# Two later layers of a two-block transformer: low halves of the weights on VectorE alone, head-norm weights in tables and copies, the compressed attention projection computed feature-major

## The reference

```
for l in range(2):
    h = rmsnorm(x, ln_mix[l])
    z = h @ w_in[l]
    (c_q 384, c_kv 128, k_rope 32, fnet 256, dq 256, dk 256, dv 256,
     hq 256, hi 256, hf_fwd 256, hf_bwd 256, hg 256, gate_logits 4096) = split(z)
    # MLA: q = rmsnorm(c_q, g_qa) @ w_uq;  k_nope, v = rmsnorm(c_kv, g_kva) @ w_ukv
    #      q, k = rmsnorm per head of 96 (g_qn, g_kn), then rope on the last 32 columns
    # diff: dq, dk: rmsnorm per head of 32 (g_qn, g_kn), rope; two softmaxes subtracted
    # hgrn: f = lb + (1 - lb) * sigmoid(hf); k = 1 - f; log f is summed along time
    # fnet: a 2-D DFT of fnet
    x = x + (sum over 4 branches of sigmoid(gate) * (o_branch @ w_branch)) @ w_out[l]
    x = x + (silu(h2 @ w_g) * (h2 @ w_u)) @ w_down[l],  h2 = rmsnorm(x, ln_ffn[l])
```

## Time and profile before

| | |
|---|---|
| median of 3 runs | 1344.58 us (1338.54 to 1344.88) |
| the profiled execution, its own time | 1347.75 us |
| its span from first to last instruction | 1346.0 us |
| mean granted TensorE clock | 0.991 |
| PE / PEld / DVE / ACT / POOL busy | 1292.8 / 1188.1 / 919.1 / 621.8 / 219.8 us |

### The profile page before, as it was taken

One profiled execution on the slowest core, in us unless ns is written; L12 is line 12 of the kernel. 1 busy time (PEld: TensorE's weight loads), 2 busy tenths in 40 slices (PEclk: granted clock), 3 DMA queues, 4 the chain that ended last, 5 costly groups with the idle time before them and its releaser, 6 DMA issues.

```text
span 1346.0 us, 22062 instructions
## 1 busy us (share of the span) xinstructions
PE 1292.8 (96%) x9180; PEld 1188.1 (88%) x9180; DVE 919.1 (68%) x1261; ACT 621.8 (46%) x1005; POOL 219.8 (16%) x175
## 2 busy tenths in 40 slices
PE   8999989999988899999999999999899998999998
PEld 7987959998877889998899998788899998999987
DVE  6868646664469977699675554579876997655553
ACT  5865445553354455343354443445463442544432
POOL 2100000000015730282000000056402730000000
PEclk9998999999999999999999999999999999999999
DMA  9522425555533424332545555434233434455552
GB/s 373 209 94 95 173 92 180 188 188 189 189 118 120 164 94 142 140 126 95 187 153 185 186 184 201 156 126 157 96 126 125 157 126 156 158 188 188 188 188 94
DMA packets 30323, 211.76 MB, mean 157 GB/s; under 512 B 3344, under 2 KB 3728, under 8 KB 5264
## 3 DMA queue, kind: packets, MB, share of 16 engines
q1 hardware_dynamic: 29936, 210.22, 43.7%
q10 hardware_dynamic: 288, 0.13, 0.0%
HBM read 209.29 MB, written 1.05 MB: 156 GB/s over the span
## 4 chain that ended last, share of the span: by engine, by line
PE 71%; DVE 18%; issue 5%; ACT 4%; POOL 1%; DMA 0%; DVEq 0%; ACTq 0%
PE bank L471 69%; DVE W L1441 1%; DVE stat L1385 1%; DVE w_lo L1469 1%; DVE x_lo L1578 1%; DVE stat L1386 1%; DVE stat L1387 1%; ACT w_hi L1024 1%; PE bank L744 1%; DVE W L1795 1%; DVE xs L1961 1%; DVE W L1428 1%; PE bank L555 1%; DVE junk L1959 1%; POOL w_lo L981 1%
## 5 line engine op out<-in xcount | busy, mean ns | idle before, releaser
L1469 DVE TENSOR_TENSOR w_lo<-ring,w_hi 128x2048 fp32r<-128x2048 f32 x157 | 366.5, 2334 | 261.1 <-ACT w_hi L1024 260.9
L1024 ACT ACTIVATE w_hi<-ring 128x1024 fp32r<-128x1024 f32 (+1 forms) x364 | 361.9, 1044 | 222.9 <-PE bank L471 211.5
L471 PE MATMUL bank<-x_hi,w_lo 128*128 128x256 f32 x1776 | 248.5, 282 | 7.4 <-POOL w_lo L981 6.3
L471 PE MATMUL bank<-x_hi,w_hi 128*128 128x256 f32 x1776 | 253.7, 284 | 0.1
L471 PE MATMUL bank<-x_lo,w_hi 128*128 128x256 f32 x1776 | 247.6, 280 | 2.2 <-DVE x_lo L1578 2.2
L471 PEld LDWEIGHTS bank<-x_hi,w_lo 128*128 128x128 f32 x1776 | 226.0, 189 | 9.5 <-POOL w_lo L981 7.2
L981 POOL TENSOR_TENSOR w_lo<-ring,w_hi 128x1024 fp32r<-128x1024 f32 (+1 forms) x48 | 115.7, 2414 | 703.3 <-ACT w_hi L1024 701.4
L471 PEld LDWEIGHTS bank<-x_hi,w_hi 128*128 128x128 f32 x1776 | 227.4, 189 | 2.2 <-DVE x_hi L1566 0.7
L471 PEld LDWEIGHTS bank<-x_lo,w_hi 128*128 128x128 f32 x1776 | 225.3, 188 | 4.2 <-DVE x_lo L1578 3.9
L471 PE MATMUL bank<-W 128*128 128x128 f32 (+4 forms) x716 | 122.4, 329 | 9.4 <-DMA const<-constants 5.7
L471 PEld LDWEIGHTS bank<-W 128*128 128x128 f32 (+3 forms) x716 | 96.1, 188 | 25.9 <-issue 6.6
(11 more groups left out here) (240 smaller groups left out, 1350.7 us busy)
## 6 DMA issues: line engine op xcount, KB each, us to landing
ring<-weight_pieces SPq DMA_DIRECT2D x191, 1024.0 KB, 4.8
const<-constants SPq DMA_DIRECT2D x1, 1376.5 KB, 9.3
W<-x_features SPq DMA_DIRECT2D x4, 256.0 KB, 5.4
ring<-weight_pieces SPq DMA_DIRECT2D x2, 512.0 KB, 6.2
h<-x SPq DMA_DIRECT2D x2, 512.0 KB, 11.9
W<-rg_weights SPq DMA_DIRECT2D x1, 1024.0 KB, 10.6
xs<-mem_features SPq DMA_DIRECT2D x1, 1024.0 KB, 11.1
oT<-mem SPq DMA_DIRECT2D x1, 1024.0 KB, 12.0
```

The source lines that it names most:

```text
L471: return nc.tensor.matmul(out, lhsT, rhs, start=first, stop=last)
L1024: return nc.scalar.activation(out, in_, ACT.Copy, scale=scale)
L1469: v.tensor_tensor(w_lo[:, q % SPLITS, 0:n], raw(pp)[:, 0:n], w_hi[:, q % SPLITS, 0:n].bitcast(F32), ALU.subtract).then_inc(s_weight_low, 1)
```

## The change

1. **Low parts.** All of them on VectorE. GpSimd's `split_ahead` and its semaphore go.
2. **Norms.** At the six norms that are not loaded from memory, ScalarE alone makes all of `x_hi` (four banks), VectorE only `x_lo`. The first half of the product after a norm takes its passes in the order: for each k `w_hi*x_hi` and `w_lo*x_hi`, then all of `w_hi*x_lo`.
3. **Projection `a`** is computed feature-major, so that `aturn` goes. ScalarE writes it with its weight column straight from the bank, and squares it; the sums of squares come from eight products with a column of ones (`ss`); the factor is applied when `uq` and `ukv` leave their banks.
4. **Head norms.** ScalarE makes the squares. The nope part of the weights is applied as a scale of the `zturn` copies; the rope part is folded into cosine and sine tables, which GpSimd makes ahead (`rope_tables`).
5. **Order of the front**: `a`, `f` half 0, `kr`, `f` half 1, `forget`, `b`, `znorm`, `c` half 0, `bnorm`, `zturn`; `c` half 1, both `e`, `bturn`, `fnet`, `hg` and the scans become filler between the attention heads, ahead of the gates.
6. **Forget gates** in one step `forget`: sigmoid, affine, 1 - f and log on ScalarE, the clamp on VectorE. `hq` is written for one direction by VectorE and copied for the other by ScalarE.
7. **Final norm of the first block and first norm of the later ones** take their roots together: `h` times the gain goes to `xs`, is squared there, and ScalarE scales it back into `h`.
8. The last piece of `down` and `wd` closes the banks by column half. The warm-up matmuls no longer wait for the identity. The bounds and lambda products (`params`) move in among the `up` projections.

The diff, cut to its core:

```diff
-            by = "pool" if name in ("b", "hg", "kr", "c", "e", "f") else "dve"
-            return [("proj", name, l, j, piece(n, by)) for j in js]
+            return [("proj", name, l, j, piece(n)) for j in js]
...
-            steps += proj("a", l) + proj("b", l)
-            steps.append(("aturn", l))
-            steps += proj("hg", l, (0,)) + proj("kr", l, (0,), KT * 32 + 96)
+            a, f0 = proj("a", l), proj("f", l, (0,))
+            steps += a + f0 + proj("kr", l, (0,), KT * 32 + 96)
+            steps += proj("f", l, (1,)) + [("forget", l)] + proj("b", l)
             c = proj("c", l)
-            steps += [c[0], ("znorm", l), c[1]]
-            steps.append(("bturn", l))
-            steps += proj("f", l)
-            steps.append(("zturn", l))
+            steps += [("znorm", l), c[0], ("bnorm", l), ("zturn", l)]
             e = proj("e", l)
-            steps += [e[0], ("logf", l), e[1], ("fnet", l)]
...
+                   [[c[1]], [e[0]], [e[1], ("bturn", l)], [("fnet", l)], [hg[0], ("scan", l, 0)], [gates[0], ("scan", l, 1)], [gates[1], ("scan", l, 2)],
+                    [gates[2], ("scan", l, 3)], [gates[3], gates[4]], [gates[5]], [gates[6], gates[7]]], 0, True)
...
+                        bank = fill(f"ss{l}", "m")
+                        for i, ks in enumerate(((0, 1, 2), (3,))):
+                            for tt in range(TT):
+                                for k in ks:
+                                    ins = mm(bank[:, 2 * i + tt:2 * i + tt + 1], sq[:, k, tt * P:(tt + 1) * P], ones_col, k == ks[0], k == ks[-1])
...
-                        for j in (0, 2):
...
+                        if name not in LOADED:
+                            for j in range(KT // 2):
                                 bank = bank2(wait_filled(act, f"{name}.{j}.0"))
                                 for k in (2 * j, 2 * j + 1):
                                     ins = copy(x_hi[:, k, :], bank[:, k % 2, :], gain[:, k:k + 1])
-                            ins.then_inc(s_norm_high, 1)
+                                ins.then_inc(s_norm_all, 1)
...
+                        if name == "a" and j == 0 and l == 0:
+                            act.wait_ge(s_rs, rs_of["ln_mix_0"])
+                            for tt in range(TT):
+                                copy(h[:, tt, :], xs[:, tt, :], col("rs.final", TT)[:, tt:tt + 1]).then_inc(s_h_normed, 1)
...
+                elif kind == "forget":
+                    link(nc.scalar.activation(at(A_KK, 4 * S), at(A_KK, 4 * S), ACT.Sigmoid))
+                    for hd in range(4):
+                        ins = nc.scalar.activation(F[:, hd, :], kk[:, hd, :], ACT.Identity, scale=om[:, c:c + 1], bias=lb[:, c:c + 1])
+                    ins.then_inc(s_affine, 1)
+                    act.wait_ge(s_affine, l + 1)
+                    for hd in range(4):
+                        ins = nc.scalar.activation(kk[:, hd, :], kk[:, hd, :], ACT.Identity, scale=nom[:, c:c + 1], bias=om[:, c:c + 1])
+                    ins.then_inc(s_hgrn_k, 1)
                     act.wait_ge(s_f, l + 1)
                     nc.scalar.activation(at(A_F, 4 * S), at(A_F, 4 * S), ACT.Ln).then_inc(s_log_f, 1)
...
-                        for tt in range(TT):
-                            for c in range(2):
+                        for c in range(2):
+                            for tt in range(TT):
```

More of the change, by code:

```diff
@@ L82 @@
 V_LB = V_QA + 4 * L2
[L83 removed]
+V_ZG = V_LB + 4 * L2
+V_SIZE = V_ZG + 2 * L2
 R_FINAL = 0
@@ L301, in piece @@
                 split.append((pieces, n))
-                low.append((by, 1 + sum(b == by for b, _ in low)))
             pieces += 1
@@ L506, in gemm, with product @@
                 pe.wait_ge(s_weight_high, 2 * q + 1)
-                passes = [(hi, x_hi), (hi, x_lo), (lo, x_hi)] if parts is None else [(hi, x_hi), (lo, x_hi), (hi, x_lo)]
-                first_half = 0 if ks else KT // 2
-                ks = ks or range(KT)
+                passes = [(hi, x_hi), (hi, x_lo), (lo, x_hi)]
+                def product(half, k, w, x, first, last):
+                    lhsT, rhs = (w[:, k, half * P:(half + 1) * P], x[:, k, :]) if form == "feat" else (x[:, k, half * P:(half + 1) * P], w[:, k, :])
+                    return mm(bank[:, half * 256:half * 256 + n], lhsT, rhs, first, last)
                 for half in range(2):
@@ L512, in gemm @@
                         between()
-                    cut = slice(half * P, (half + 1) * P)
+                    if half == 0 and parts:
+                        order = ks or range(KT)
+                        if ks:
+                            pe.wait_ge(s_weight_high, 2 * (q + 1))
+                        for n_k, k in enumerate(order):
+                            if parts(k):
+                                pe.wait_ge(*parts(k)[0])
+                            if n_k == KT // 2 and not ks:
+                                pe.wait_ge(s_weight_high, 2 * (q + 1))
+                            product(0, k, hi, x_hi, n_k == 0, False)
+                            if n_k == 0:
+                                wait_low(pe, q)
+                            product(0, k, lo, x_hi, False, False)
+                        for n_k, k in enumerate(order):
+                            if parts(k):
+                                pe.wait_ge(*parts(k)[1])
+                            product(0, k, hi, x_lo, False, n_k == KT - 1)
+                        continue
                     for i, (w, x) in enumerate(passes):
@@ L1183, in _ @@
+                        drains(ins, job)
+                    elif name == "e" and j == 1:
+                        hq = at(A_HQ, 2, 2, S)
+                        wait_drained(act, job)
+                        for o in range(2):
+                            ins = copy(hq[64 * (1 - o):64 * (1 - o) + 64, :, o, :], hq[64 * o:64 * o + 64, :, o, :])
+                        ins.then_inc(s_hq, 1)
                     elif name == "hg":
@@ L2086, in pack_vectors @@
     parts.append(lb)
+    for l in range(L2):
+        for n in ("mla_g_qn_2", "mla_g_kn_2"):
+            parts.append(np.concatenate([a[n][l][:64], np.ones(P - 64, np.float32)])[:, None])
     out = np.ascontiguousarray(np.concatenate(parts, 1))
```

432 lines of the change are left out of this document (208 added, 224 removed).

## The result

| | before | changed |
|---|---|---|
| median of 4 runs | 1344.73 us (1338.54 to 1348.01) | 1369.51 us (1366.67 to 1372.09) |
| ratio, 95% interval | | 1.0189 (1.0147 to 1.0232) |
| span of the profiled execution | 1346.0 us | 1368.6 us |
| mean granted TensorE clock | 0.991 | 0.981 |

What follows compares the result with a forecast made beforehand. TensorE, busy 1292.8 of 1346.0 us, was taken as the bound, so new waits are paid in full. Terms 4.8 + 0.7 + 3 - 0.7 + 6.2 + 10.5 + 0.5 = +25 us on 1344.6 gave 1370 us, eight-in-ten range 1337 to 1386.

Steps and rivals of the forecast that it cites:

- the front of layer 0: From `a` to the first gate: new pauses, 5.8 us at `f` half 0 among them, make it 6.2 us longer.
- `forget` ahead of the high part of `b` half 1: Later layers' fronts: ScalarE runs `forget` for 8.2 us before that high part, so TensorE waits 5.5 us.
- The table load: In `forget`: two loads of 1.28 us each on the path, with no further drain of about 1.38 us.
- `zturn`, `e` half 0, `fnet`: Later in the front: TensorE waits 2.0 us (plus 1.0 at the first score), 4.7 us and 5.8 us.
- Low clock: Three norm pauses of 2.7 us may each cost a low-clock spell: 3 us with others, between 0 and 10.
- every pause at low clock: Rival: four pauses per layer and three at norms cost 1.6 us each, 18 us instead of 3: 1385 us; chance 0.11.
- slow spells "that are many": Whole program: low-clock spells that are many, or none, would show the forecast wrong.
- Norms: Root 1.6 us later at three norms, 4.8 us; next piece's low part at `norm_mlp_g` +0.7; last `x_lo` 0.9 earlier.
- Ends of the attention parts: Rest of the two attention parts after the heads: no change, 0 us, was forecast.
- Start: Program start: warm-up matmuls moved ahead of the wait gain 0.7 us, between 0 and 2.
- freed VectorE wins: Rival: without GpSimd's low parts stretching VectorE's chain, the fronts' idle time goes by half or more: 1335 us; chance 0.22.
- two low parts: Front, kernel before: GpSimd makes two from 405.43 to 410.3, while a 4-column VectorE instruction takes 2.37 us, otherwise 0.16.

Runs made afterwards that it cites:

- experiment 1: Changed kernel with the high and low part of `b` half 1 made ahead of `forget` in both later layers: 1367.43 us, ratio 1.0179.
- experiment 10: Changed kernel measured and profiled once more with no edit: 1368.28 us, ratio 1.0163, profiled span 1357.8 us.
- Experiment 6: Kernel before with part 1 of the change alone, all low parts on VectorE: 1363.13 us, ratio 1.0134.
- experiment 11: Changed kernel with part 1 alone undone, low parts of six projections and the first two gates on GpSimd again: 1368.27 us, ratio 1.0169.
- Experiment 12: Kernel of experiment 8 plus `c` half 1 before the first score and `fnet` cut around `hg` (1315.03 us), with the front's low parts on GpSimd again: 1336.80 us.
- experiments 3: Changed kernel with the norms' high parts divided between ScalarE and VectorE again: 1358.96 us, ratio 1.0124.
- 4: Changed kernel with `fnet` moved behind the product of `hg` in both later layers: 1357.20 us, ratio 1.0116.
- experiment 5: Changed kernel with the high part of `f` half 0 made ahead of the wait for the roots: 1364.10 us, ratio 1.0143.
- 7: Changed kernel with the front cut finer: `b` half 1 split ahead of `forget`; `forget`, `znorm`, `bnorm` each in two: 1358.27 us, ratio 1.0099.
- experiment 8: Changed kernel with the moves of experiments 3, 4, 5 and 7 all together: 1331.49 us, ratio 0.9898.

## Why the prediction was right, and where its terms were not

The median was predicted at 1370 and is 1369.5. The mechanism is the one that was predicted: waits for ScalarE's high parts and VectorE's chains, at the places named. The closeness is luck in part, because errors of 4 to 9 us cancel. In the front of layer 0 the seven pauses add up to 19.5 us, where the forecast's are 5.8 + 5.5 + 2.0 + 1.0 + 4.7 + 5.8 = 24.8. The slow spells, which its sum for the front leaves out, add up to 9.2. Together that is 19.5 + 9.2 - 24.8 = 3.9 us more than forecast, which is what the table shows (+10.1 against +6.2).

- **`forget` ahead of the high part of `b` half 1.** Predicted 5.5 us of pause, measured 6.32 in both layers, ended by ScalarE's high part; experiment 1 shows the cause. `forget` took 8.85 and not 8.2 us: each of its two groups of four copies takes 2.08, where I took 1.71 from the earlier trace rows.
- **The table load.** I went by the row, 1.28 us and nothing behind it, and the rows of `forget` are the same: the second load starts at 432.80, where the copies ahead of it end, and the logarithm 1.29 us later. By the Trainium skill (ScalarE: Activation LUTs, What ACT_TABLE_LOAD costs) each switch has a drain of a further 1.38 us or so; the trace does not agree.
- **`zturn`, `e` half 0, `fnet`.** Places right, sizes too large: 3.0, 4.7 and 5.8 us predicted, 1.7, 2.9 and 3.5 measured in layer 0. Each pause is the difference of two queues' counts, and each pause ahead of it shortens it (with the one at `b` half 1 gone, experiment 1 has 3.60 at `zturn`). That this is why they came out small is argued, not shown.
- **Low clock: the term that was mis-sized.** "I take 3 us for these and others together." The 3 us fit the norms, where the pauses at `ln_ffn_0` and `ln_ffn_1` had a slow spell of 1.6 us each behind them. For the fronts, where the forecast itself had pauses of 4.7 to 5.8 us, nothing was left. Measured there, each as the time of the products against their time at full clock: 1.7 us behind `f` half 0, 2.5 behind `b` half 1, 2.0 behind `e` half 0 and 3.0 within `fnet` in layer 0; 2.1, 1.7 and 2.5 behind the last three in layer 1. The same stretches as in the earlier trace rows (there 0.96 and 0.98), in the changed kernel:

```profile
380.00:500.00 120.00, 99.90 (x689) 90.83 (x688) 64.13 (x124) 66.82 (x124) 0.00 (x0) 0.91 0.29 106
875.00:987.00 112.00, 94.78 (x673) 86.08 (x672) 60.91 (x119) 60.84 (x116) 0.00 (x0) 0.92 0.31 113
```

  Over the whole program the mean granted clock says (1 - 0.981) x 1368.6 - (1 - 0.991) x 1346.0 = 13.9 us more than before, some of it while TensorE stood still. The forecast's own sign of being wrong, slow spells "that are many", did come: the clock falls to the lower level 11 times, and 6 times before. My rival "every pause at low clock", with 18 us, was nearer in this term; it missed the total because the pauses were smaller than counted.
- **Norms.** The mechanism is right (root later by 1.3, predicted 1.6; last `x_lo` ends 1.2 us earlier after the transposes). Undoing the step gave 10.5 us in the medians and, with the quicker rate taken out, 8.2 in the trace, against 4.8 + 0.7 + 3 = 8.5 in the sum: right within the noise. The waits for the next piece's low part, 1.5 us behind two norms, were not counted at `ln_mix_1` and stood with 0.7 at `norm_mlp_g`.
- **Ends of the attention parts.** -4.0 us that I had not: in layer 0, `wout` starts with one pause of 1.39 us where it had 0.75 and 1.55 with a slow spell, and runs at the quicker rate of experiment 10. Together with the smaller pauses they pay for the clock.
- **Start.** -0.4 against -0.7. The first product starts 2.7 us earlier, but waits 2.34 us for its operands first, has further short waits and runs at the lower clock level for its first 3 us, which it did not before.
- **The rival "freed VectorE wins"** is refuted twice. Experiment 6 makes the low parts' move cost 18 us in the old order, and experiment 11 makes it worth nothing in the new. Its argument was sound for what it looked at: 2.76 against 0.69 us for the same instruction, with and without GpSimd's low parts beside it. The Trainium skill (GPSIMD Engine Reference, Specifications) has the two engines share their SBUF interfaces, with contention for VectorE instructions in a 2-port mode or with two inputs there; the trace agrees for this instruction, which has two. What it left out is that VectorE's queue is in order, so that a head norm of 11.6 us ahead of a low part (experiment 6) costs more than a slow low part beside it. Experiment 12 shows the same argument winning, by 22 us, once the blocks are cut.
- **A misreading without effect.** The forecast calls the two GpSimd instructions of the earlier trace rows two low parts. They are the two halves of one; the times taken from them hold.

That the losses add up was itself tested: experiments 3, 4, 5 and 7 alone gave 10.5, 12.3, 5.4 and 11.2 us, 39.4 in sum, and together 38.0. So close an agreement is partly luck, since each difference has the noise of two medians: from the second measurement of the changed kernel (1368.28, experiment 10) it would be 34.6 and 36.8.

## What to carry to other kernels

Where engines run their queues in order, ask of every block that is longer than the other engine's cover (here 5.4 us of a piece) what stands behind it. Cutting the blocks and putting the urgent splits between their parts gave 11 us without one instruction fewer, while moving a whole block gave 2 us, within the noise, or cost 7. A pause of several us costs twice, once as a pause and again as a slow spell behind it (here 1.6 to 3.0 us), so count both. And apply an expected gain alone before trusting it, because its sign can depend on the order around it.

## What the runs showed of the hardware

- TensorE's stream of 256-column matmuls ran at 0.907 or 0.943 us for eight, at granted clock 1.00, in stretches of up to 110 us, and at other places in two executions of one program. What sets the rate is open. It is worth up to 10 us per execution here, the same size as the spread of the runs.
- After pauses of 6.32, 4.97 and 2.91 us, and in `fnet` after two of 1.62 and 1.90 close together, the next products ran at the lower clock level for 3 to 6 us. After the single pause of 1.42 us at the first score they did not, but behind one of 1.46 at 79.1 us they did (mean granted clock 0.66 from 79 to 84 us).
- Between 2.4 and 3.1 us the length of the pause did not decide. In the changed kernel the pauses of 2.46 and 2.62 us at `ln_ffn_0` and `ln_ffn_1` were followed by such a spell (mean granted clock 0.72 from 693 to 699 us and from 1182 to 1188) and the one of 2.46 at `norm_cross_g` was not (1.00 from 163 to 169). In experiment 5 all three were. In experiment 8 the pauses of 2.5 and 3.1 us were followed by one in layer 0 (0.72) and not in layer 1 (1.00). Each pause of 3.6 us or more behind the first product was, in all these traces.
